# Two transitions with two norms each: fewer weight slabs rounded on the way, the normed rows recorded in two parts, sums over two tiles at a time

## The chip, the cores and the metric

The kernel runs on one core of a Trainium2 chip. The time is that of the device, in microseconds (us), for one execution; lower is better. TensorE (PE in the profile) multiplies, VectorE (DVE) and ScalarE (ACT) do elementwise work, GpSimd (POOL) does elementwise work that touches no PSUM, and SyncE (SP) issues the DMAs. Each engine takes its instructions in the order in which the kernel wrote them, and waits at an instruction until the semaphores that it names have been raised.

## The reference, cut to what matters

One layer of a first network (a mixer with three branches, then a gated feed-forward part), followed by two layers of a second network, on 512 positions of width 1024. Of all this the change touches the places between the parts, where a norm closes one and a norm opens the next:

```python
x = x + rms_norm(merged @ w_o, g_post_mix)      # transition "f": norm 1 (N1) of the product
hf = rms_norm(x, g_pre_ffn)                     #   and norm 2 (N2) of the new x
f_gate, f_up = jnp.split(hf @ w_ffn_in, 2, axis=-1)
f = (jax.nn.silu(f_gate) * f_up) @ w_ffn_out
x = x + rms_norm(f, g_post_ffn)                 # transition "a0": N1 of the product,
h = rmsnorm(x, norm_w) * (1.0 + scale) + shift  #   N2 of the new x, then layer 0 of network 2
proj = h @ w_in
...
x = x + gate * (merged @ w_out)                 # transition "a1": one norm only, to layer 1
```

`rms_norm(x, g)` is `x * rsqrt(mean(x * x) + EPS) * g` over the width.

## The kernel before, in words

Activations are held transposed: a tile is 128 of the 1024 width rows by 512 positions, so a width-1024 array is 8 tiles (k = 0 to 7), and a mean over the width is a sum over partitions and tiles. Each product is computed to near fp32 accuracy from two parts, a rounded one and a rest (`Hhi`, `Hlo` of the activations, `w_hi`, `w_lo` of the weights), in three matmuls per tile (`tile_sums`). The weights arrive as slabs of 8 tiles of 128x128: a DMA brings `w_raw`, ACT rounds it to `w_hi` (`round_weights`), and POOL subtracts to get `w_lo` (`rest_weights`), in pieces of `n` of the slab's 8 tiles. `cut_to(s, n)` records this for all slabs up to s; `self.cut` is the next slab not yet rounded. Slots are few (four in the ring, one called `w_fifth`, and two or three more at a transition, `wf`, `wa`).

A recording layer decides the order: a generator per product yields as it goes, and background tasks (`later`) count these yields down and record a piece of their own work when their count is spent (`tick`). `yield 12` in a task thus means: twelve steps of the product later; in `halves` a step is two tiles.

A transition (`both`) computes the last parts of the old product in two halves of 256 positions, half 0 and half 1 (`halves(first_parts)`), and then the first four parts of the next product, half 0 and half 1 (`halves(next_parts, deep=4)`), where the four parts share each activation tile k. After each half of the old product its task `two_norms` starts:

- `norm_end(N1)`: PE sums the squares over partitions (matmuls with `ones`, `row_sums`), ACT takes the root (`root`, writes `rstds`), DVE inverts it (`inverse`), PE spreads it over the partitions (transposes with `ident`, `row_spread`).
- `onto`: for each tile k, DVE multiplies O by the inverse root (`o_times`) and adds it to `XR` (`x_add`); ACT squares the new x (`square`), and POOL adds the square to N2's accumulator (`add_square`, the second norm has `by="pool"`; tile 7 is not added but summed directly by PE).
- `norm_end(N2)`, the same for the second norm.
- `normed`: for each tile k, DVE scales x (`h_scaled`, tile `hu`), ACT rounds it to `Hhi` (`h_rounded`), and DVE or, for k = 3, 5 and 7, POOL makes `Hlo` (`h_rest`). Three buffers `hu` take turns. In a0 there is a shift too: ACT adds it (`n<-n,mod`) before POOL's rows.

The accumulator of N2 is `nt_178` in the listings of f. In half 1 of the old product every slab that is finished (`over` counts them) lets the next be rounded, from the second one on in `both` (`early=1`). Before the next product's half 0 the task of half 0 is recorded to its end (`self.finish(tasks[0])`).

Of the kernel before, what the change touches and what calls it, by code (L numbers as in the profile page):

```python
# [171 lines left out]
def program(nc, A, out):  # L172
# [202 lines left out]
    class Order:  # L375
# [172 lines left out]
                        done -= 512  # L548
                        yield 1

        def halves(self, parts, before=None, after=None, deep=1, early=2):
            kept, over = {}, 0
            for h, c in enumerate(HALF):
                for n0 in range(0, len(parts), deep):
                    group = range(n0, n0 + deep)
                    if h == 0 and deep > 1:
                        for n in group:
                            for k in parts[n][1]:
                                kept[n, k] = self.tile(calm=True)
                    if before and n0 == 0:  # L560
                        before(h)
                    if h and deep > 1 and n0 == 0:
                        self.cut_to(self.cut + 1)
                    bank = [open_[h] if open_ else self.wide.take() for _, _, _, _, open_ in parts[n0:n0 + deep]]
                    for x, k in enumerate(parts[n0][1]):
                        for n in group:
                            X, ks, key, evac, open_ = parts[n]
                            if h == 0 and deep == 1:
                                kept[n, k] = self.tile()
                            b, tile, ends = bank[n - n0], kept[n, k], k == ks[-1]  # L570
                            names = [(*key, c.start)] * ends + [("slab", tile.s)] * (h and tile.ends)
                            self.tile_sums(banks[b][:, 0:256], tile, X, k, c, k == ks[0] and not open_, ends, self.freed[b], names)
                            if h and tile.ends:
                                self.slab_done(tile.s)
                                self.old = self.sent
                                self.send()
                                over += 1
                                if deep == 1 and over > early:
                                    self.cut_to(self.cut, 4)
                            if (x * deep + n) % 2:  # L580
                                yield 1
                            if ends:
                                X.spent = sums.by(*key, c.start)
                                self.freed[b] = evac(banks[b][:, 0:256], sums.by(*key, c.start), c)
                if after:
                    after(h)
# [44 lines left out]
        def normed(self, c, N, x_ready, hs, scale, shift, H_free, *before, by=None, gap=0, odds=(4, 6)):  # L631

            gone = [None] * len(hs)
            h = c.start // 256

            def rest(k, odd):
                who = (by or "pool") if odd else "dve"
                self.h_rest(N, k, c, hs[k % len(hs)], shift and shift(k), odd, who)
                done = (dve_norm if who == "dve" else pool_norm).by("rest", N.name, k, h)
                gone[k % len(hs)] = done  # L640
                self.H.h[k] = tuple(act_norm.by("h", N.name, k, i) if i <= h else None for i in range(2))
                old = self.H.l[k]
                self.H.l[k] = (done, None) if h == 0 else (old[0], done)

            for k in range(KT):
                if k == 2 and gap:
                    yield gap
                t = hs[k % len(hs)]
                self.h_scaled(N, k, c, t, scale(k), [N.m, x_ready(k, c), gone[k % len(hs)], before])
                if k:  # L650
                    rest(k - 1, k in odds)
                self.h_rounded(N, k, c, t, shift and shift(k), [H_free, before])
            self.norm_read(N, dve_norm.by("scaled", N.name, KT - 1, h))
            rest(KT - 1, True)
# [432 lines left out]

        def onto(self, c, name, dst, o_ready, N1, N2, x_ready, *before):
            h = c.start // 256
            for k in range(KT + 1):  # L1090
                if k < KT:
                    self.o_times(name, dst, k, c, N1, [N1.m, o_ready[k, h]])
                if k:
                    self.x_add(name, dst, k - 1, c, before)
                    x_ready[k - 1, h] = dve_o.by("x", name, k - 1, h)
                    self.norm_add(N2, k - 1, XR[:, k - 1, c], x_ready[k - 1, h], c)
            self.norm_read(N1, dve_o.by("times", name, KT - 1, h))

        def two_norms(self, h, name, dst, o_ready, N1, N2, x_ready, hs, scale, shift, H_free, *before):
            c = HALF[h]  # L1100
            yield 2 if h else 1
            yield from self.norm_end(N1, c, 3 if h else 1)
            self.onto(c, name, dst, o_ready, N1, N2, x_ready, *before)
            yield 9 if h else 12
            yield from self.norm_end(N2, c, 1 if h else 3)
            yield from self.normed(c, N2, lambda k, c: x_ready[k, c.start // 256], hs, scale, shift, H_free, *before, gap=8)

        def both(self, first_parts, next_parts, chain, name, *slots_free):
            self.pump()
            self.ready_sqrt()  # L1110
            self.wide.past(self.main.which)
# [2 lines left out]
            self.send()  # L1114
            self.retire(slots)
            H_free = self.H.spent
            self.run(self.halves(first_parts, after=lambda h: tasks.append(self.later(chain(h, H_free))), early=1))
            self.run(self.halves(next_parts, before=lambda h: self.finish(tasks[h]), deep=4))
            self.main.past([self.wide.which[(self.wide.turn - 1) % 8]])
            return self.gone(slots)  # L1120

# [200 lines left out]
        def walk(self):  # L1322
# [119 lines left out]
            for n in range(3):  # L1442
# [2 lines left out]
                [(MS, range(KT), ("o", n), evac(n), None) for n in range(3, KT)],  # L1445
                [(H, range(KT), ("raw", i, x), (lambda o, done, c, i=i, x=x: self.raw(i, x, o, done, c)), None) for i in range(2) for x in range(2)],
                lambda h, H_free: self.two_norms(h, "O", O, o_ready, n_post, n_pre, x_ready, hu[h], lambda k: P("g_pre_ffn", k), None, H_free, x_again),
                "f", Y.spent)
            norm_done += [H.h[KT - 1][1], H.l[KT - 1][1]]
            F = Split(each(Fhi), each(Flo), FT)  # L1450
            for i in range(2):
# [85 lines left out]
        def layer(self, L, H, x_ready, x_parts, x_chain, x_slots_free, layer_free):  # L1537
# [3 lines left out]
            begun = self.both(x_parts,  # L1541
                              [(H, range(KT), (t, L, 0, g), (self.to_k if t == "bk" else self.to_q)(L, 0, g), None)
                               for t, g in (("bk", 0), ("bk", 1), ("bk", 2), ("bq", 0))],
                              x_chain, f"a{L}", *x_slots_free)
            x_free = dict(x_ready)
            begun += [H.h[KT - 1][1], H.l[KT - 1][1]]
            self.begun = begun
# [704 lines left out]
    class Dve(Order):  # L2252
# [316 lines left out]

        def o_times(self, name, dst, k, c, N1, points):  # L2570
            self.wait_ge(*points)
            self.tt(dst[:, k, c], dst[:, k, c], N1.r, ALU.mult).then_inc(*dve_o("times", name, k, c.start // 256))

        def x_add(self, name, dst, k, c, points):
            h = c.start // 256
            self.wait_ge(dve_o.by("times", name, k, h), *points)
            self.tt(XR[:, k, c], XR[:, k, c], dst[:, k, c], ALU.add).then_inc(*dve_o("x", name, k, h))

        def first_gated(self, i):
            self.wait_ge(act_ffn.by("tanh", i))  # L2580
# [445 lines left out]
```

## Time and profile before

| | |
|---|---|
| median of 3 runs | 2541.43 us (2541.1 to 2542.52) |
| the profiled execution | 2543.01 us, of which its span is 2541.2 us |
| PE busy | 2497.3 us, 98% of the span |
| POOL busy | 1152.4 us, 45% |
| DVE busy, ACT busy | 1167.8 us, 1060.3 us |

Read it as follows: PE is busy nearly throughout, and the other engines less than half of the time, so the kernel's time is PE's work plus what PE waits. The average says nothing of a single transition, in which short dependent steps go round all four engines.

### The profile page before, as it was taken

To read this page: it belongs to the slowest core of one execution; us is meant where nothing else is said; L and a number is where in the kernel's file an instruction comes from. 1 tells how busy PE (TensorE), PEld (TensorE's weight loads), DVE (VectorE), ACT (ScalarE), POOL (GpSimd) and SP (SyncE) were. 2 spreads that over 40 slices of the span, in tenths; PEclk is the share of its full clock that TensorE was granted. 3 is DMA by queue.
4 is the path that set the end of the run, shared out by engine and by line. 5 is a ranking of instruction groups with operands and counts; after the bars stand their busy time and mean duration, and the time that the engine had idled before them with its cause. 6 is when DMAs were issued, how large, how long until landed. Compare 5 with 4: busy or idle time off the path is not lost.

```text
span 2541.2 us, 33038 instructions
## 1 busy us (share of the span) xinstructions
PE 2497.3 (98%) x13246; PEld 2145.8 (84%) x13246; DVE 1167.8 (46%) x2376; ACT 1060.3 (42%) x2026; POOL 1152.4 (45%) x682
## 2 busy tenths in 40 slices
PE   8999999999999999999999999999999999999998
PEld 7788888888888888889888888888898888898887
DVE  7672477755415782104243455522243345544313
ACT  4472498952325332325433333333344333333322
POOL 4354354554446355445444445534444334444442
PEclk9999999999999999999999999999999999999999
DMA  5223211035433453222222222222322222222222
GB/s 201 67 100 109 68 42 34 34 116 199 154 115 113 159 194 124 100 100 75 99 83 83 83 79 87 92 83 99 115 84 84 83 83 75 92 79 88 92 100 75
DMA packets 71769, 250.47 MB, mean 99 GB/s; under 512 B 7872, under 2 KB 12736, under 8 KB 71232
## 3 DMA queue, kind: packets, MB, share of 16 engines
q1 hardware_dynamic: 71616, 248.35, 28.2%
q8 instruction: 105, 1.72, 0.3%
q14 instruction: 48, 0.39, 0.0%
HBM read 246.22 MB, written 2.10 MB: 98 GB/s over the span
## 4 chain that ended last, share of the span: by engine, by line
PE 86%; DVE 6%; ACT 5%; POOL 1%; issue 1%; DMA 0%; SPq 0%; DVEq 0%; ACTq 0%; POOLq 0%
PE bank L1736 84%; PE bank L1746 2%; ACT PP L1954 1%; POOL w_lo L2802 1%; ACT pt_hi L1954 1%; ACT QQ L1954 1%; ACT w_hi L1954 1%; DVE pt_lo L2256 0%; DVE rk_lo L2256 0%; DVE nt L2256 0%; DVE Y L2256 0%; DVE XR L2256 0%; DVE C L2256 0%; DVE PP L2509 0%; DMA XR<-in_x 0%
## 5 line engine op out<-in xcount | busy, mean ns | idle before, releaser
L2802 POOL TENSOR_TENSOR w_lo<-w_raw,w_hi 128x1024 fp32r<-128x1024 f32 (+1 forms) x319 | 761.7, 2392 | 882.3 <-ACT w_hi L1954 882.0
L1736 PE MATMUL bank<-Hhi,w_hi 128*128 128x512 f32 (+1 forms) x1676 | 656.5, 392 | 4.5 <-DVE XC L2264 4.5
L1736 PE MATMUL bank<-Hhi,w_lo 128*128 128x512 f32 (+1 forms) x1676 | 647.6, 386 | 0.0
L1736 PE MATMUL bank<-Hlo,w_hi 128*128 128x512 f32 (+1 forms) x1676 | 647.5, 386 | 0.0
L1954 ACT ACTIVATE w_hi<-w_raw 128x1024 fp32r<-128x1024 f32 (+1 forms) x319 | 326.1, 1027 | 123.1 <-DMA w_raw<-in_wa 81.7
L1736 PEld LDWEIGHTS bank<-Hhi,w_lo 128*128 128x128 f32 x1676 | 315.6, 188 | 65.0
L1736 PEld LDWEIGHTS bank<-Hhi,w_hi 128*128 128x128 f32 x1676 | 316.0, 189 | 61.5 <-DVE XC L2264 4.9
L1736 PEld LDWEIGHTS bank<-Hlo,w_hi 128*128 128x128 f32 x1676 | 316.4, 189 | 56.1
L2802 POOL TENSOR_TENSOR w_fifth_lo<-w_fifth_raw,w_fifth_hi 128x1024 fp32r<-128x1024 f32 (+1 forms) x79 | 190.7, 2415 | 224.8 <-ACT w_fifth_hi L1954 224.8
L1736 PE MATMUL bank<-Hhi,w_fifth_hi 128*128 128x512 f32 x404 | 162.6, 402 | 0.0
L1736 PE MATMUL bank<-Hhi,w_fifth_lo 128*128 128x512 f32 x404 | 157.9, 391 | 0.0
L1736 PE MATMUL bank<-Hlo,w_fifth_hi 128*128 128x512 f32 x404 | 157.7, 390 | 0.0
L2827 POOL TENSOR_SCALAR PP<-PP,small 128x128 f32<-128x128 f32 (+3 forms) x128 | 65.8, 533 | 75.3 <-DVE small L2256 74.9
L1736 PE MATMUL bank<-Y,w_hi 128*128 128x512 f32 x304 | 93.5, 389 | 0.0
L1954 ACT ACTIVATE w_fifth_hi<-w_fifth_raw 128x1024 fp32r<-128x1024 f32 (+1 forms) x79 | 81.6, 1036 | 26.5 <-DMA w_fifth_raw<-in_wa 21.2
L1736 PE MATMUL bank<-w_hi,Hhi 128*128 128x256 f32 (+2 forms) x296 | 89.9, 304 | 0.0
L1736 PEld LDWEIGHTS bank<-Hhi,w_fifth_lo 128*128 128x128 f32 x404 | 75.8, 188 | 16.6
L1736 PE MATMUL bank<-w_hi,Hlo 128*128 128x256 f32 (+2 forms) x296 | 89.6, 303 | 0.0
L1736 PE MATMUL bank<-w_lo,Hhi 128*128 128x256 f32 (+2 forms) x296 | 89.5, 302 | 0.0
L1736 PEld LDWEIGHTS bank<-Hhi,w_fifth_hi 128*128 128x128 f32 x404 | 76.0, 188 | 12.5 <-issue 0.2
L1736 PEld LDWEIGHTS bank<-Hlo,w_fifth_hi 128*128 128x128 f32 x404 | 76.2, 189 | 12.3
L2539 DVE CUSTOM_DVE_ANT_0 wm<-wm,c 128x1024 f32<-128x1024 f32 x48 | 78.8, 1646 | 6.6 <-DMA wm<-in_w_ada 6.4
(413 smaller groups left out, 4913.6 us busy)
## 6 DMA issues: line engine op xcount, KB each, us to landing
w_raw<-in_wb SPq DMA_DIRECT2D x169, 512.0 KB, 3.4
w_raw<-in_wa SPq DMA_DIRECT2D x139, 512.0 KB, 3.3
wm<-in_w_ada SPq DMA_DIRECT2D x48, 512.0 KB, 4.4
w_fifth_raw<-in_wb SPq DMA_DIRECT2D x42, 512.0 KB, 3.4
w_fifth_raw<-in_wa SPq DMA_DIRECT2D x35, 512.0 KB, 3.2
wa_raw<-in_wb SPq DMA_DIRECT2D x5, 512.0 KB, 5.3
XR<-in_x SPq DMA_DIRECT2D x4, 512.0 KB, 8.1
w1k<-in_w1k SPq DMA_DIRECT2D x1, 2048.0 KB, 12.5
```

The lines of the kernel that those rows point to most:

```text
L1736: return self.e.matmul(o, lhs, rhs, start=start, stop=stop)
L1746: return self.e.transpose(o, i, ident[0:n, 0:n])
L1954: return self.e.activation(o, a, func, **kw)
L2539: self.e.tensor_tensor_reduce(x, x, cc[l][:, :], .5, 0., ALU.mult, ALU.add, mod[:, l, n:n + 1]).then_inc(*dve_mod("row", l, n))
L2802: self.e.tensor_tensor(x.lo[:, k:k + n, :], x.raw[:, k:k + n, :], f(x.hi[:, k:k + n, :]), ALU.subtract).then_inc(*w_rest(s, k))
L2827: self.e.tensor_scalar(p, p, r[:, n:n + 1], 1., ALU.mult, ALU.mult).then_inc(*pool_nsa("p", u, n))
```

## The change

In `halves`, slabs are rounded in half 1 of the old product only when `over` is in `cuts`: 2 in f and a1, 2 and 3 in a0. Two slabs more are rounded inside `two_norms` of half 1, between `norm_end(N1)` and `onto`. `normed` gives way for 3 steps before row 4 of half 0; before the next product only rows 0 to 3 need have been recorded. `o_times` and `x_add` work on two tiles at once. The sums of half 0's second norm are recorded two steps earlier, and its spread one step earlier still.

```diff
-        def halves(self, parts, before=None, after=None, deep=1, early=2):
+        def halves(self, parts, before=None, after=None, deep=1, cuts=()):
...
-                                if deep == 1 and over > early:
+                                if over in cuts:
                                     self.cut_to(self.cut, 4)
...
             for k in range(KT):
                 if k == 2 and gap:
                     yield gap
+                if k == 4 and h == 0:
+                    yield 3
+                self.emitted = k + 1
...
         def onto(self, c, name, dst, o_ready, N1, N2, x_ready, *before):
             h = c.start // 256
-            for k in range(KT + 1):
-                if k < KT:
-                    self.o_times(name, dst, k, c, N1, [N1.m, o_ready[k, h]])
-                if k:
-                    self.x_add(name, dst, k - 1, c, before)
-                    x_ready[k - 1, h] = dve_o.by("x", name, k - 1, h)
-                    self.norm_add(N2, k - 1, XR[:, k - 1, c], x_ready[k - 1, h], c)
-            self.norm_read(N1, dve_o.by("times", name, KT - 1, h))
+            for k in range(0, KT, 2):
+                self.o_times(name, dst, k, c, N1, [N1.m, o_ready[k, h], o_ready[k + 1, h]])
+                self.x_add(name, dst, k, c, before)
+                for j in (k, k + 1):
+                    x_ready[j, h] = dve_o.by("x", name, k, h)
+                    self.norm_add(N2, j, XR[:, j, c], x_ready[j, h], c)
+            self.norm_read(N1, dve_o.by("times", name, KT - 2, h))
...
             yield from self.norm_end(N1, c, 3 if h else 1)
+            if h:
+                self.cut_to(self.cut + 1)
             self.onto(c, name, dst, o_ready, N1, N2, x_ready, *before)
-            yield 9 if h else 12
-            yield from self.norm_end(N2, c, 1 if h else 3)
+            yield 9 if h else 10
+            yield from self.norm_end(N2, c, 1 if h else 2)
...
-            self.run(self.halves(first_parts, after=lambda h: tasks.append(self.later(chain(h, H_free))), early=1))
-            self.run(self.halves(next_parts, before=lambda h: self.finish(tasks[h]), deep=4))
+
+            def before(h):
+                if h:
+                    self.finish(tasks[1])
+                    return
+                while self.emitted < 4:
+                    tasks[0][1] = next(tasks[0][0])
+
+            self.emitted = 0
+            self.run(self.halves(first_parts, after=lambda h: tasks.append(self.later(chain(h, H_free))), cuts=cuts))
+            self.run(self.halves(next_parts, before=before, deep=4))
```

How this moves instructions is shown at three places, all in transition f; a0 has the same pattern. First POOL's order, from the last two additions of half 0's second norm (`nt_178`) to the first two of half 1's. Before:

```order
L2807 TENSOR_TENSOR nt_178<-nt_178,nt_176 128x256
L2802 TENSOR_TENSOR w_lo<-w_raw,w_hi 128x512 x4
L2802 TENSOR_TENSOR w_fifth_lo<-w_fifth_raw,w_fifth_hi 128x512 x2
L2802 TENSOR_TENSOR w_lo<-w_raw,w_hi 128x512 x2
L2813 TENSOR_TENSOR Hlo<-hu_179,Hhi 128x256
L2813 TENSOR_TENSOR Hlo<-hu_181,Hhi 128x256
L2813 TENSOR_TENSOR Hlo<-hu_180,Hhi 128x256
L2807 TENSOR_TENSOR nt_178<-nt_178,nt_175 128x256
```

The same place on POOL after the change:

```order
L2823 TENSOR_TENSOR nt_178<-nt_178,nt_176 128x256
L2818 TENSOR_TENSOR w_lo<-w_raw,w_hi 128x512 x2
L2829 TENSOR_TENSOR Hlo<-hu_179,Hhi 128x256
L2829 TENSOR_TENSOR Hlo<-hu_181,Hhi 128x256
L2829 TENSOR_TENSOR Hlo<-hu_180,Hhi 128x256
L2818 TENSOR_TENSOR w_lo<-w_raw,w_hi 128x1024
L2818 TENSOR_TENSOR w_fifth_lo<-w_fifth_raw,w_fifth_hi 128x1024
L2823 TENSOR_TENSOR nt_178<-nt_178,nt_175 128x256
```

Three slabs' worth of rests have left the place ahead of half 0's `Hlo` rows 3, 5 and 7, and two whole slabs stand now between row 7 and half 1's additions.

Second ACT's order, from the last rounded rows of half 0 to the first square of half 1's second norm (`nt_178<-XR`); `rstds<-bank` is the root of half 1's first norm. Before:

```order
L1954 ACTIVATE Hhi<-hu_181 128x256
L1954 ACTIVATE Hhi<-hu_179 128x256
L1954 ACTIVATE Hhi<-hu_180 128x256
L1954 ACTIVATE Hhi<-hu_181 128x256
L1954 ACTIVATE Hhi<-hu_179 128x256
L1954 ACTIVATE Hhi<-hu_180 128x256
L1954 ACTIVATE rstds<-bank,eps 128x2
L1954 ACTIVATE nt_178<-XR 128x256
```

The same place on ACT after the change:

```order
L1968 ACTIVATE Hhi<-hu_181 128x256
L1968 ACTIVATE Hhi<-hu_179 128x256
L1968 ACTIVATE rstds<-bank,eps 128x2
L1968 ACTIVATE Hhi<-hu_180 128x256
L1968 ACTIVATE Hhi<-hu_181 128x256
L1968 ACTIVATE Hhi<-hu_179 128x256
L1968 ACTIVATE Hhi<-hu_180 128x256
L1968 ACTIVATE w_hi<-w_raw 128x1024
L1968 ACTIVATE w_fifth_hi<-w_fifth_raw 128x1024
L1968 ACTIVATE nt_178<-XR 128x256
```

The root has moved ahead of rows 4 to 7, and two roundings stand ahead of the squares.

Third PE's order in half 1 of the old product of f, at the sums (`ones`) of half 0's second norm; `w_fifth` and `w` are two slabs, one behind the other. Before:

```order
L1736 MATMUL bank<-MShi,w_lo 128x256
L1736 MATMUL bank<-ones,nt_178 128x1 x2
L1736 MATMUL bank<-ones,nt_177 128x1 x2
L1736 MATMUL bank<-MShi,w_hi 128x256
L1736 MATMUL bank<-MSlo,w_hi 128x256
```

After the change:

```order
L1750 MATMUL bank<-MShi,w_fifth_lo 128x256
L1750 MATMUL bank<-ones,nt_178 128x1 x2
L1750 MATMUL bank<-ones,nt_177 128x1 x2
L1750 MATMUL bank<-MShi,w_hi 128x256
L1750 MATMUL bank<-MSlo,w_hi 128x256
```

The sums stood behind the third tile of slab `w` and stand now ahead of its first: three tiles (nine matmuls) earlier, and four tiles in a0. The spread that belongs to them has moved along; nothing else has moved on PE in any transition. On DVE the 16 products and 16 sums over 256 positions in each of f and a0 have become half as many over 2x256; on SP nothing has moved.

## Rows read from the trace of the kernel before

**Rows 1.** The page: span, and busy time by engine.
```profile
span 2541.2 us, 33038 instructions
...
PE 2497.3 (98%) x13246; PEld 2145.8 (84%) x13246; DVE 1167.8 (46%) x2376; ACT 1060.3 (42%) x2026; POOL 1152.4 (45%) x682
```

**Rows 2.** Timeline of PE in f: start, busy, instruction, idle before it and its releaser.
```profile
804.02 0.95 PE L1736 MATMUL bank<-ones,nt 128*128 128x1 f32 x8
...
809.93 0.28 PE L1736 MATMUL bank<-MShi,w_lo 128*128 128x256 f32 x1
811.15 0.35 PE L1736 MATMUL bank<-Hhi,wf_hi 128*128 128x256 f32 x1 [0.94 <-ACT Hhi L1954]
...
813.03 0.95 PE L1736 MATMUL bank<-ones,nt 128*128 128x1 f32 x8
...
818.28 0.43 PE L1746 MATMUL bank<-ident,rstds 128*128 128x128 f32 x2 [2.05 <-DVE rstds L2290]
...
826.23 1.05 PE L1736 MATMUL bank<-ones,nt 128*128 128x1 f32 x8 [1.05 <-POOL nt L2807]
```

**Rows 3.** Timeline of PE in a0.
```profile
1176.77 0.95 PE L1736 MATMUL bank<-ones,n 128*128 128x1 f32 x8
...
1182.54 0.28 PE L1736 MATMUL bank<-Hhi,wa_hi 128*128 128x256 f32 x1
...
1190.71 0.43 PE L1746 MATMUL bank<-ident,rstds 128*128 128x128 f32 x2 [3.42 <-DVE rstds L2290]
...
1198.94 0.95 PE L1736 MATMUL bank<-ones,n 128*128 128x1 f32 x8
```

**Rows 4.** Windows: stretch, its us, PE, PEld, DVE, ACT, POOL, granted clock, DMA.
```profile
1190.00:1200.00 10.00, 9.29 (x66) 9.29 (x67) 6.99 (x17) 3.87 (x11) 5.15 (x7) 0.83 0.00 1
...
1860.00:1870.00 10.00, 10.00 (x86) 10.00 (x85) 4.95 (x12) 4.60 (x10) 6.79 (x6) 1.00 0.31 107
```

**Rows 5.** Timeline of ACT in f, and one row of a0.
```profile
786.43 1.06 ACT L1954 ACTIVATE wf_hi<-wf_raw 128x1024 fp32r<-128x1024 f32 x1
...
817.07 0.81 ACT L1954 ACTIVATE Hhi<-hu 128x256 fp32r<-128x256 f32 x2 [1.41 <-DVE hu L2264]
817.79 0.24 ACT L1954 ACTIVATE rstds<-bank,eps 128x2 f32<-128x2 f32 x1
...
1189.80 0.51 ACT L1954 ACTIVATE n<-n,mod 128x256 f32<-128x256 f32 x1
```

**Rows 6.** Timeline of POOL in f.
```profile
785.81 7.68 POOL L2802 TENSOR_TENSOR wf_lo<-wf_raw,wf_hi 128x1024 fp32r<-128x1024 f32 x3
798.24 5.14 POOL L2807 TENSOR_TENSOR nt<-nt,nt 128x256 f32<-128x256 f32 x6 [4.74 <-ACT nt L1954]
804.47 5.42 POOL L2802 TENSOR_TENSOR w_lo<-w_raw,w_hi 128x512 fp32r<-128x512 f32 x4 [1.09 <-ACT w_hi L1954]
...
815.54 1.59 POOL L2813 TENSOR_TENSOR Hlo<-hu,Hhi 128x256 fp32r<-128x256 f32 x2
...
821.04 5.14 POOL L2807 TENSOR_TENSOR nt<-nt,nt 128x256 f32<-128x256 f32 x6 [2.36 <-ACT nt L1954]
```

**Rows 7.** Timeline of DVE in f.
```profile
779.12 0.69 DVE L2256 TENSOR_TENSOR nt<-nt,nt 128x512 f32<-128x512 f32 x1 [4.75 <-ACT nt L1954]
783.67 10.11 DVE L2256 TENSOR_TENSOR nt<-nt,nt 128x256 f32<-128x256 f32 x4 [3.86 <-ACT nt L1954]
...
797.29 0.42 DVE L2256 TENSOR_TENSOR XR<-XR,O 128x256 f32<-128x256 f32 x1
...
799.51 0.63 DVE L2256 TENSOR_TENSOR XR<-XR,O 128x256 f32<-128x256 f32 x1
...
831.18 0.87 DVE L2264 SCALAR_TENSOR_TENSOR hu<-XR,par,bank 128x256 f32<-128x256 f32 x2
```

**Rows 8.** Timeline of POOL in a0.
```profile
1170.99 5.16 POOL L2807 TENSOR_TENSOR n<-n,n 128x256 f32<-128x256 f32 x6 [7.15 <-ACT n L1954]
...
1193.46 5.14 POOL L2807 TENSOR_TENSOR n<-n,n 128x256 f32<-128x256 f32 x6 [2.35 <-ACT n L1954]
```

More of the change, by code:

```diff
@@ L1102, in two_norms, with both @@
             yield from self.norm_end(N1, c, 3 if h else 1)
+            if h:
+                self.cut_to(self.cut + 1)
             self.onto(c, name, dst, o_ready, N1, N2, x_ready, *before)
-            yield 9 if h else 12
-            yield from self.norm_end(N2, c, 1 if h else 3)
+            yield 9 if h else 10
+            yield from self.norm_end(N2, c, 1 if h else 2)
             yield from self.normed(c, N2, lambda k, c: x_ready[k, c.start // 256], hs, scale, shift, H_free, *before, gap=8)
-        def both(self, first_parts, next_parts, chain, name, *slots_free):
+        def both(self, first_parts, next_parts, chain, name, cuts, *slots_free):
             self.pump()
@@ L1447, in walk @@
                 lambda h, H_free: self.two_norms(h, "O", O, o_ready, n_post, n_pre, x_ready, hu[h], lambda k: P("g_pre_ffn", k), None, H_free, x_again),
-                "f", Y.spent)
+                "f", (2,), Y.spent)
             norm_done += [H.h[KT - 1][1], H.l[KT - 1][1]]
@@ L1543, in layer @@
                                for t, g in (("bk", 0), ("bk", 1), ("bk", 2), ("bq", 0))],
-                              x_chain, f"a{L}", *x_slots_free)
+                              x_chain, f"a{L}", (2,) if L else (2, 3), *x_slots_free)
             x_free = dict(x_ready)
@@ L2571, in o_times @@
             self.wait_ge(*points)
-            self.tt(dst[:, k, c], dst[:, k, c], N1.r, ALU.mult).then_inc(*dve_o("times", name, k, c.start // 256))
+            x = dst[:, k:k + 2, c]
+            self.tt(x, x, N1.r.unsqueeze(1).broadcast_to([128, 2, 256]), ALU.mult).then_inc(*dve_o("times", name, k, c.start // 256))
         def x_add(self, name, dst, k, c, points):
@@ L2576, in x_add @@
             self.wait_ge(dve_o.by("times", name, k, h), *points)
-            self.tt(XR[:, k, c], XR[:, k, c], dst[:, k, c], ALU.add).then_inc(*dve_o("x", name, k, h))
+            x = XR[:, k:k + 2, c]
+            self.tt(x, x, dst[:, k:k + 2, c], ALU.add).then_inc(*dve_o("x", name, k, h))
         def first_gated(self, i):
```

## The prediction

> **What bounds the kernel now.** I read the page first: PE is busy 2497.3 of 2541.2 us [rows 1], so what counts is where PE waits, and in a transition who releases it. The timelines of PE show this. In f it idles 0.94 us for the first `Hhi`, 2.05 us for the spread of half 1's first norm and 1.05 us for half 1's second sums [rows 2]; in a0 it idles 3.42 us for the same spread, and none at the second sums [rows 3]. The other timelines say who is late. Half 1's root stands on ACT behind all eight `Hhi` rows of half 0: the root starts at 817.79, right behind the pair of 817.07, though PE's sums for it stood at 813.03 [rows 2, 5]. The rows themselves wait for POOL, whose `Hlo` rows start only at 815.54, behind the roundings that began at 804.47 [rows 6]. And PE's wait at 826.23 ends with POOL's six additions, 821.04 plus 5.14 us [rows 2, 6]. In a1 PE is busy without a gap in half 1 (10.00 of 10.00 us) [rows 4].
>
> After a transition PE has no slack to recover what it lost, so the shift at half 1's second sums, 826.23 in f and 1198.94 in a0, is what reaches the end. I price both.
>
> **Unit costs.** 86 matmuls fit into 10.00 us [rows 4], 0.12 us each: a tile is 0.36 us, the four tiles of one k 1.44. The block of eight `ones` matmuls: 0.95 busy, 0.9 from start to start [rows 2]. Root, inverse, spread: from 817.79 to 818.28 [rows 2, 5], 0.5. DVE scales a row in 0.39 (two in 0.87 busy, which overlap) [rows 7]. ACT rounds a row in 0.41 [rows 5]. A sum over 256 positions shows 0.42 busy, 0.34 apart; one over 512 shows 0.69 [rows 7], so I take 0.6 for a pair. POOL: 2.4 to 2.56 for a whole slab (7.68 for three) [rows 6], I take 2.4; an addition 0.885 apart (5.14 for six, the last 0.74) [rows 6].
>
> **Half 0's sums earlier.** PE reaches them in f at 804.02 less 9 x 0.12, 802.94 [rows 2]. POOL's additions ended at 803.38 [rows 6]. With pairs the third square comes a little later than it did, since x arrives in twos (two more 0.3 us steps, partly hidden behind POOL): I take 0.4 late, 803.8. PE waits 0.85 there. In a0: 1176.77 less 1.44 is 1175.33, and POOL is ready at 1170.99 + 5.16 + 0.4 = 1176.55: 1.2 [rows 3, 8]. The old product of f then ends 0.85 later, at 810.05 + 0.85 = 810.9 instead of 810.05 (last matmul 809.93) [rows 2]. As the rows are ready by then, the 0.94 us wait disappears: H begins at 810.9 instead of 811.15. In a0, where nothing was idle, it begins at 1182.54 + 1.2 = 1183.75 [rows 3].
>
> **The root out of the queue.** After one k (1.44) and the sums (0.9) ACT can take the root: 813.25 in f, 1186.1 in a0; only rows 0 to 3 stand ahead of it, and those are done. The inverse is there at 813.75 and 1186.6, and PE asks for the spread six tiles after the sums, 2.16 us: 815.4 and 1188.25. The waits of 2.05 and 3.42 are gone. PE is 2.9 us ahead of before in f and 2.5 in a0 at this point. The 18 tiles that follow (6.5 us) bring it to half 1's second sums at 822.2 and 1195.0.
>
> **The roundings in front of half 1's additions.** Now the other side. Rows 4 to 7 of half 0 follow the inverse. In f they take four scalings and two rests on DVE, 2.65 us with one wait for ACT: 816.4. In a0 ACT is the longer one, four rows at 0.41 and three shifts at 0.51 [rows 5] less overlap, 3.1 us: 1189.7. Only then do ACT and POOL come to the two whole slabs. This work stood elsewhere before and cost nothing there but the waits above; POOL is now idle between 807 and 812 us and busy afterwards.
>
> How long it takes depends on how DVE and POOL get on when both read two tensors of SBUF. In the trace four such DVE sums over 256 positions, next to whole-slab rests on POOL, took 10.11 us, 2.5 each, against 0.42 alone [rows 7]: each waited out one POOL instruction. Next to POOL's short additions it was 0.63 [rows 7]. That speaks for taking turns, one whole instruction each. The Trainium skill (SBUF — State Buffer, the part on the shared port pair) says the same as a rule: it is an exclusive lock held for the whole instruction, and the later one fully blocks. By that rule the taking of turns below would hold for the pairs, which nothing in the trace of before shows, and the sum is the first one; if the engines merely slowed each other, it is the second.
>
> - Taking turns, f: POOL's row 7 ends at 817.15, the first `x_add` pair 0.6 later, 817.75; then slab 2.4, pair 0.6, slab 2.4, pair 0.6: 823.75; one addition 0.74, the last pair 0.6, five additions at 0.885: 829.5. Against 826.19 that is **+3.3**.
> - Taking turns, a0: row 7 ends at 1190.5, first pair 1191.1, slab-pair-slab-pair 1197.1, addition and pair 1198.45, five additions 1202.85. PE's sums stood at 1198.94 [rows 3]: **+3.9**.
> - Without turns, f: ACT's rounding (1.06 busy, 0.96 apart [rows 5]) lets POOL start at 817.4, two slabs 822.2, six additions 827.5: +1.3. In a0: 1190.7, 1195.5, 1200.8: +1.9.
>
> I take the first, since its 2.5 us rows are of the same two kinds of instruction. PE would idle about 7.3 us in f and 7.9 in a0.
>
> **The clock.** After 3.42 us of idleness in a0 the granted clock is 0.83 over the next 10 us [rows 3, 4]: a third of that stretch at the lower of its two levels (1.2 instead of 2.4 GHz), 1.7 us lost. After 2.05 us in f nothing of the kind came; the stretch shows its matmuls at the usual spacing [rows 2]. With 7 us of idleness I expect the loss in f too, **+1.7**, and in a0 the same again in place of the old one, 0. Bounds: no new loss, or twice as much in each.
>
> **What costs nothing.** The 16 instructions fewer on DVE in each of f and a0 save perhaps 0.06 each, on an engine that waits for POOL here anyway. One slab fewer is rounded ahead at the end of f and a0, and two in a1; PE needs 24 matmuls over 512 positions per slab after the transition, at twice 0.12 some 5.5 us, and POOL 2.4, so the cover is four rounded slabs; gone, it would cost 2.4. In a1 a sum of half 1 now stands ahead of rows 4 to 7 and delays them by about 1.2 us; they are not needed until the old product is finished, some 4 us later, and PE shows no gap [rows 4].
>
> **Sum.** 3.3 + 3.9 + 1.7 = 8.9 us. The profiled execution took 2543.01 us with a span of 2541.2 and would become 2551.9; against the median of the runs, 2541.43, it gives **2550.3 us**.
>
> **Rivals.**
> - *The engines only slow each other* (second sum, 1.3 + 1.9 = 3.2, or 4.9 with the clock in f): 2544.6 to 2546.3, not to be told from no change, which is 0.2% or 5.1 us here. For it: `x_add` at 0.63 next to short additions reads as sharing too. Against it: the 10.11 us row.
> - *The roundings slip in before half 1's additions matter*, and the change is faster. It decides at the start of the additions: earlier than 821.04 in f and 1193.46 in a0 [rows 6, 8]. Working back 4.8 for POOL and about 1.0 for ACT, half 0's row 7 would have to be rounded by 815.2 and 1187.6; I have 816.4 and 1189.7. If the two slabs cost nothing at all, the additions would end near 824.0 and 1196.7, 2.2 less each, and a0's 1.7 of lower clock might go: 6.1 us, 2535.3 us. For it: the root's waits really vanish. Against it: the order on POOL, which is strict.
> - *Slabs run short after the transition*: one or two waits of 2.4 us on top of the sum, 2552.7 to 2555. Little speaks for it, as POOL needs less than half of PE's time per slab.
>
> **How the numbers follow.** Taking turns 0.55, slowing each other 0.25, faster 0.12, short slabs 0.08. Low end: the second sum, without the delay at half 0's sums (0.85 and 1.2), is about 1.2 us, 2542.6; I go down to 2542. High end: 8.9 with twice the clock loss in each transition, 3.4 more: 2553.7; I take 2554. Slower by over 0.2% needs more than 5.1 us: taking turns nearly always, short slabs, and a small part of the sharing case: 0.64. Within 0.2%: 0.25. Faster: 0.11.
>
> **What would show it.** In the profile after: no wait of PE for `rstds` of half 1's first norm (right: the root left the queue). A wait of 0.5 to 1.3 us at half 0's second sums. The largest wait of each transition at half 1's second sums, released by POOL's `nt` or `n`, 5 us and more. Whole-slab `w_lo` on POOL from about 817.5 and 1191, with `x_add` rows of 2 us and more beside it: turns; of 1 us: sharing. A stretch of lower clock behind both. Wrong would be: the second sums of half 1 earlier than 826.23 and 1198.94.

## The result, and the profile after

| | median us | lowest to highest | ratio to the kernel before, 95% interval |
|---|---|---|---|
| kernel before, beside it | 2541.10 | 2540.14 to 2542.52 | |
| changed kernel | 2557.15 | 2555.14 to 2557.32 | 1.0057 [1.0047, 1.0068] |

The change makes the kernel slower: by 0.57% or 14.5 us as the ratio has it, by 16 us as the two medians have it. The page's lines that answer to [rows 1]:

```profile
span 2555.5 us, 32988 instructions
...
PE 2503.3 (98%) x13246; PEld 2152.7 (84%) x13246; DVE 1163.3 (46%) x2344; ACT 1058.9 (41%) x2019; POOL 1155.3 (45%) x675
```

The span grew by 14.3 us and PE's busy time by 6.0 with the same 13246 instructions. So some 8 us are waits of PE, and the 6 us in which the same instructions were busy longer I put down to a slower clock, which the windows below show. To find the places I measure from spread to spread: the pair of `ident` matmuls of half 0's first norm stands in each transition at the same place of PE's order.

| us | start to f | f to a0 | a0 to a1 | a1 to end |
|---|---|---|---|---|
| before | 795.54 | 372.75 | 682.36 | 690.55 |
| after | 796.32 | 379.55 | 690.36 | 689.27 |
| difference | +0.78 | **+6.80** | **+8.00** | -1.28 |

I leave the outer columns out. The first grew by a longer time at the lower clock before 100 us, far ahead of any changed instruction. The last lost such a stretch: in a1 the granted clock was 0.72 from 1850 to 1856 us before, behind a wait of 0.79 us, and 1.00 from 1866 to 1872 us after, behind a wait of 0.80 us. The rest is in f and a0. PE's rows in both, after (timeline, to be read against [rows 2, 3]; `nt` is f, `n` is a0):

```profile
805.41 1.05 PE L1750 MATMUL bank<-ones,nt 128*128 128x1 f32 x8 [1.53 <-POOL nt L2823]
807.72 0.63 PE L1760 MATMUL bank<-ident,rstds 128*128 128x128 f32 x2
...
818.38 0.38 PE L1760 MATMUL bank<-ident,rstds 128*128 128x128 f32 x2
831.74 1.87 PE L1750 MATMUL bank<-ones,nt 128*128 128x1 f32 x8 [6.52 <-POOL nt L2823]
...
1185.12 1.05 PE L1750 MATMUL bank<-ones,n 128*128 128x1 f32 x8 [2.05 <-POOL n L2823]
...
1195.41 0.95 PE L1750 MATMUL bank<-ones,n 128*128 128x1 f32 x8
...
1212.56 1.87 PE L1750 MATMUL bank<-ones,n 128*128 128x1 f32 x8 [7.26 <-POOL n L2823]
```

The waits of 2.05 and 3.42 us for `rstds` are gone: the root left the queue. In their place stand 1.53 and 2.05 us at half 0's second sums and 6.52 and 7.26 us at half 1's, all released by POOL. The 1.87 us of the eight `ones` matmuls, 0.95 at full clock, shows what follows such a wait. In windows (stretch, its us, PE, PEld, DVE, ACT, POOL, granted clock, DMA):

```profile
800.00:815.00 15.00, 13.47 (x101) 13.27 (x100) 7.18 (x15) 7.48 (x21) 7.29 (x8) 0.89 0.38 130
...
830.00:845.00 15.00, 13.26 (x86) 13.05 (x87) 5.40 (x14) 6.51 (x15) 6.63 (x7) 0.74 0.01 2
```

The same windows before:

```profile
800.00:815.00 15.00, 13.90 (x114) 13.32 (x114) 10.90 (x20) 10.84 (x28) 13.48 (x12) 1.00 0.44 145
830.00:845.00 15.00, 15.00 (x112) 14.35 (x112) 4.79 (x12) 7.16 (x15) 4.63 (x4) 1.00 0.17 54
```

A clock of 0.89 over 15 us is a fifth to a quarter of it at the lower level. The chain that makes PE wait, on POOL and then on DVE (timelines of f, after):

```profile
798.99 6.37 POOL L2823 TENSOR_TENSOR nt<-nt,nt 128x256 f32<-128x256 f32 x6 [4.71 <-ACT nt L1968]
...
820.33 2.64 POOL L2818 TENSOR_TENSOR w_lo<-w_raw,w_hi 128x1024 fp32r<-128x1024 f32 x1 [0.21 <-ACT w_hi L1968]
822.92 2.86 POOL L2818 TENSOR_TENSOR w_fifth_lo<-w_fifth_raw,w_fifth_hi 128x1024 fp32r<-128x1024 f32 x1
825.73 5.95 POOL L2823 TENSOR_TENSOR nt<-nt,nt 128x256 f32<-128x256 f32 x6
```

```profile
820.00 0.69 DVE L2270 TENSOR_TENSOR XR<-XR,O 128x512 f32<-128x512 f32 x1
820.61 0.68 DVE L2270 TENSOR_TENSOR O<-O,bank 128x512 f32<-128x512 f32 x1
821.32 2.20 DVE L2270 TENSOR_TENSOR XR<-XR,O 128x512 f32<-128x512 f32 x1
823.44 0.68 DVE L2270 TENSOR_TENSOR O<-O,bank 128x512 f32<-128x512 f32 x1
824.15 2.17 DVE L2270 TENSOR_TENSOR XR<-XR,O 128x512 f32<-128x512 f32 x1
```

Two `x_add` pairs (`XR<-XR,O`) begin while POOL is in a whole slab and last until it is through it, 2.2 us against 0.69: the two take turns. And POOL's six additions take 6.37 and 5.95 us, where [rows 6] shows 5.14 twice. In a0 half 0's six take longer too, where [rows 8] shows 5.16:

```profile
1178.54 6.53 POOL L2823 TENSOR_TENSOR n<-n,n 128x256 f32<-128x256 f32 x6 [7.29 <-ACT n L1968]
```

### The profile page after: what moved, and what is told of

It reads as the page before. It is cut to its first block, busy times and chain, and to the rows that moved or that the text cites. A ratio compares the mean times of both kernels' runs of the same rounds, so it can differ in the third digit from the quotient of the medians.

```text
span 2555.5 us, 32988 instructions
## 1 busy us (share of the span) xinstructions
PE 2503.3 (98%) x13246; PEld 2152.7 (84%) x13246; DVE 1163.3 (46%) x2344; ACT 1058.9 (41%) x2019; POOL 1155.3 (45%) x675
## 4 chain that ended last, share of the span: by engine, by line
PE 87%; DVE 6%; ACT 5%; POOL 1%; issue 1%; DMA 0%; SPq 0%; DVEq 0%; POOLq 0%; ACTq 0%
PE bank L1750 85%; PE bank L1760 2%; ACT PP L1968 1%; ACT pt_hi L1968 1%; ACT QQ L1968 1%; ACT w_hi L1968 1%; DVE pt_lo L2270 0%; DVE rk_lo L2270 0%; POOL n L2823 0%; POOL nt L2823 0%; DVE nt L2270 0%; DVE Y L2270 0%; DVE C L2270 0%; DVE PP L2523 0%; POOL w_lo L2818 0%
## 5 line engine op out<-in xcount | busy, mean ns | idle before, releaser
L2818 POOL TENSOR_TENSOR w_fifth_lo<-w_fifth_raw,w_fifth_hi 128x1024 fp32r<-128x1024 f32 x77 | 190.6, 2475 | 224.6 <-ACT w_fifth_hi L1968 224.6
L1968 ACT ACTIVATE w_fifth_hi<-w_fifth_raw 128x1024 fp32r<-128x1024 f32 x77 | 81.4, 1057 | 25.0 <-DMA w_fifth_raw<-in_wa 20.9
```

Source lines behind the costliest of these rows:

```text
L1968: return self.e.activation(o, a, func, **kw)
L2818: self.e.tensor_tensor(x.lo[:, k:k + n, :], x.raw[:, k:k + n, :], f(x.hi[:, k:k + n, :]), ALU.subtract).then_inc(*w_rest(s, k))
```

## Experiments

The change has five edits: fewer cuts; half 0's rows in two parts; half 0's second sums sooner; pairs; two slabs ahead of half 1's additions. E1 to E3 take one off the changed kernel, E4 leaves only the first two, E5 and E6 make one of these two alone in the kernel before, E7 to E9 add one of the other three to E4. E10 to E12 try to go on from E6. Each median is over 9 or 10 executions; the kernel before stood at 2542.1 to 2542.5 beside them. The changed kernel was not run beside them: where they are set against it, its 2557.15 is that of the result, beside which the kernel before stood at 2541.10. Each ratio carries about 0.1% (2.5 us) either way, so a difference of 2 or 3 us between two kernels of this table is not clear of noise.

| | kernel | median us | ratio to before, 95% interval |
|---|---|---|---|
| E1 | changed, no slabs ahead | 2546.88 | 1.0015 [1.0006, 1.0024] |
| E2 | changed, no pairs | 2549.25 | 1.0024 [1.0015, 1.0034] |
| E3 | changed, sums late | 2549.42 | 1.0027 [1.0017, 1.0037] |
| E4 | fewer cuts, two parts | 2537.08 | 0.9977 [0.9967, 0.9988] |
| E5 | before, two parts | 2540.93 | 1.0001 [0.9991, 1.0010] |
| E6 | before, fewer cuts | 2536.89 | 0.9982 [0.9973, 0.9992] |
| E7 | E4, sums early | 2539.64 | 0.9990 [0.9981, 1.0000] |
| E8 | E4, pairs | 2541.65 | 0.9997 [0.9987, 1.0006] |
| E9 | E4, slabs ahead | 2546.43 | 1.0016 [1.0007, 1.0026] |
| E10 | E6, no cuts | 2549.79 | 1.0030 [1.0021, 1.0040] |
| E11 | E6, half 1's sums later | 2537.42 | 0.9978 [0.9969, 0.9988] |
| E12 | E6, products in pairs | 2537.93 | 0.9986 [0.9977, 0.9996] |

**E1, the slabs.**

```diff
-            if h:
-                self.cut_to(self.cut + 1)
             self.onto(c, name, dst, o_ready, N1, N2, x_ready, *before)
```

> The changed kernel without the two slabs that are rounded ahead of half 1's additions; nothing is left out of the computation, the slabs are rounded at their old places behind. Theory A (the slabs stand in front of the additions and take turns with DVE, and this is the main part of the loss): in f and in a0 the sums over half 1's additions are ready some 4 us earlier, the waits of 6.5 and 7.3 us of PE there go to 2 to 3, and the lower clock behind them goes in part; time about 2546 us (8 to 13 less than the changed kernel's 2557.15). Theory B (the pairs and the early sums of half 0 are the main part): less than 4 us less, 2553 or more. Theory C (the slabs are needed by the product that follows, and are short when rounded later): a new wait on w_hi or w_lo in the next product, and a time above 2557.

2546.88 us, 10.3 less: theory A. PE's rows at the second sums (timeline; the last is that of a0):

```profile
804.99 1.05 PE L1748 MATMUL bank<-ones,nt 128*128 128x1 f32 x8 [1.52 <-POOL nt L2821]
...
827.48 1.87 PE L1748 MATMUL bank<-ones,nt 128*128 128x1 f32 x8 [2.69 <-POOL nt L2821]
...
1204.48 1.05 PE L1748 MATMUL bank<-ones,n 128*128 128x1 f32 x8 [3.45 <-POOL n L2821]
```

The waits at half 1's fell by 3.8 us in each, and those at half 0's stayed. PE waits for weights twice in the whole run, 3.0 and 1.1 us, both at the start of the kernel (9.1 and 10.6 us), where the kernel before waits too; in the transitions there is no such wait, so theory C falls as well. But 4.4 us over the kernel before are left, which no slab explains.

**E2, the pairs.** `onto`, `o_times` and `x_add` as before the change:

```diff
-            for k in range(0, KT, 2):
-                self.o_times(name, dst, k, c, N1, [N1.m, o_ready[k, h], o_ready[k + 1, h]])
-                self.x_add(name, dst, k, c, before)
...
+            for k in range(KT + 1):
+                if k < KT:
+                    self.o_times(name, dst, k, c, N1, [N1.m, o_ready[k, h]])
+                if k:
+                    self.x_add(name, dst, k - 1, c, before)
...
```

> The changed kernel with the additions and the products with N1's row one tile at a time, as before; nothing is left out of the computation. Theory A (pairs let POOL's additions of squares begin later and run longer, since squares come in bursts of two and DVE's pair writes hold POOL up): half 0's six additions fall from 6.4 to 6.5 us back to 5.1 to 5.3, PE's waits of 1.53 us in f and 2.05 us in a0 at half 0's second sums fall to 0.3 to 0.9, and the time is about 2553 us (3 to 6 less than the changed kernel's 2557.15). Theory B (pairs cost nothing, the burst is hidden): 2556 to 2558. Theory C (pairs save): above 2558.

2549.25 us, 7.9 less: theory A in kind, and above its 3 to 6. POOL's six additions are back at 5.15 us (798.05) and PE waits 0.34 us at half 0's second sums:

```profile
803.25 1.05 PE L1751 MATMUL bank<-ones,nt 128*128 128x1 f32 x8 [0.34 <-POOL nt L2822]
...
827.59 1.87 PE L1751 MATMUL bank<-ones,nt 128*128 128x1 f32 x8 [5.32 <-POOL nt L2822]
```

The clock between 800 and 815 us is 1.00 again, and I take that for what my 3 to 6 had too little of. It is not certain to come with these waits: E7 has them too (0.33 us, and 0.51 for the spread behind) and its clock there is 0.89.

**E3, the early sums.**

```diff
-            yield 9 if h else 10
-            yield from self.norm_end(N2, c, 1 if h else 2)
+            yield 9 if h else 12
+            yield from self.norm_end(N2, c, 1 if h else 3)
```

> The changed kernel with half 0's second sums at their old place, two steps of products later, and the spread three steps behind them; nothing is left out of the computation. Theory A (the sums are asked for before POOL has them, at a clock price too): PE's waits of 1.53 us in f and 2.05 us in a0 before half 0's second sums fall to 0.5 or less, and the two-part rows still keep the root out of PE's queue: time about 2553.5 us (3 to 4 less than the changed kernel's 2557.15). Theory B (the waits at half 0's sums are made up for by the wait at half 1's, which POOL ends at a time that PE does not set): 2556.5 to 2557.5, with the wait at half 1's sums longer by what is saved. Theory C (the early sums bring the root earlier): above 2558.

2549.42 us, 7.7 less, twice what theory A gave. PE waits 0.46 at half 0's second sums and the clock is 1.00 from 800 to 815 us. The wait at half 1's stayed at 6.52 us in f, so theory B falls: what PE loses at half 0's sums puts half 1's first norm off by as much, and with it the chain that ends in half 1's second sums. Counted from f's first spread, half 1's first sums stand at 16.41 us against 19.01 in the changed kernel, and its second sums at 32.82 against 35.42: 2.6 us sooner both.

**E4, what is left.** E1, E2 and E3 in one.

> The changed kernel without the slabs ahead of half 1's additions, without the pairs and without the early sums: what is left of the change is the fewer cuts and the normed rows in two parts; nothing is left out of the computation. Theory A (the rows in two parts take away the waits of 2.05 and 3.42 us on the root, and the rest of the change is what costs): 2536 to 2539 us, 2 to 5 below the kernel before. Theory B (half 1's additions are next to be late, so the time saved at the root is given back there): 2540 to 2543, no difference to the kernel before. Theory C (fewer cuts leave slabs short in the next product): 2543 or more, with waits on w_hi or w_lo.

2537.08 us: theory A by the time, 5.4 below the kernel before. That the two parts are the reason is what E5 and E6 test.

**E5, the rows in two parts alone.**

```diff
                 if k == 2 and gap:
                     yield gap
+                if k == 4 and h == 0:
+                    yield 3
+                self.emitted = k + 1
```

and `both` with its `before` of the change.

> The kernel before with one part of the change alone: half 0's normed rows issued in two parts around half 1's root; cuts as before; nothing is left out of the computation. Theory A (the rows in two parts carry the whole gain of the run that has only them and the fewer cuts, because they take PE's waits of 2.05 and 3.42 us on the root away): PE's waits on rstds fall as in that run, 2536 to 2539 us, some 5 below the kernel before. Theory B (the fewer cuts carry the gain, by leaving DVE and POOL free of slabs near the additions): 2541 to 2543, no difference to the kernel before. Theory C (without the fewer cuts a slab comes to lie in front of the root): the wait on rstds stays, and the time is within 1 us of the kernel before.

2540.93 us, ratio 1.0001: theory B. The wait of half 1's spread on `rstds` is gone, as theory A wanted it, and yet the time stays. From f to a0 it is 372.76 us against 372.75. Where the wait went (timeline of PE, f and a0):

```profile
824.25 1.07 PE L1748 MATMUL bank<-ones,nt 128*128 128x1 f32 x8 [2.43 <-POOL nt L2819]
...
1196.74 1.47 PE L1748 MATMUL bank<-ones,n 128*128 128x1 f32 x8 [3.57 <-POOL n L2819]
```

Half 1's root runs sooner, but its additions stand on DVE behind half 0's rows 4 to 7 as before; POOL begins them at 819.08, which is 0.9 us sooner when the 1.1 us by which this run's f came sooner are taken off. So one wait of 2.43 us at the sums stands for the old ones of 2.05 and 1.05. From f to a0 PE idles 1.06 us less than before and is busy 1.07 us longer: its clock was 0.89 from 815 to 830 us, and 1.00 before.

```profile
815.00:830.00 15.00, 12.57 (x91) 12.16 (x90) 10.85 (x27) 6.92 (x19) 6.19 (x9) 0.89 0.00 1
```

**E6, the fewer cuts alone.**

```diff
-                                if deep == 1 and over > early:
+                                if over in cuts:
                                     self.cut_to(self.cut, 4)
```

with the `cuts` of the change handed to it.

> The kernel before with one part of the change alone: cuts only at the second (and, in a0, third) slab that the old product gives back; nothing is left out of the computation. Theory A (fewer roundings alone move no wait of PE, the root is late by its place in the queues): PE's waits of 2.05 and 3.42 us on rstds stay, 2541 to 2544 us. Theory B (the roundings that lay ahead of the root made it late): these waits fall by over 1 us each and the time to 2539 or less.

2536.89 us: theory B. f to a0 is 369.15 us, 3.6 less than before. The waits on `rstds` fell from 2.05 to nothing and from 3.42 to 1.02 us, with the root still behind all eight rows of half 0 on ACT (it starts at 814.05, against 817.79 before). POOL and PE in f:

```profile
804.34 2.73 POOL L2802 TENSOR_TENSOR w_lo<-w_raw,w_hi 128x512 fp32r<-128x512 f32 x2 [1.09 <-ACT w_hi L1954]
811.54 0.72 POOL L2813 TENSOR_TENSOR Hlo<-hu,Hhi 128x256 fp32r<-128x256 f32 x1 [4.47 <-ACT Hhi L1954]
```

```profile
811.34 0.95 PE L1736 MATMUL bank<-ones,nt 128*128 128x1 f32 x8
814.55 0.43 PE L1746 MATMUL bank<-ident,rstds 128*128 128x128 f32 x2
...
822.50 1.05 PE L1736 MATMUL bank<-ones,nt 128*128 128x1 f32 x8 [1.05 <-POOL nt L2807]
```

In [rows 6] POOL was in weights without a gap until 815.54, and the rows of half 0, ahead of the root on ACT, had to wait for it. Now it does one slab, and takes the first of its `Hlo` rows at 811.54, 4 us sooner.

**E7, E8, E9: the other three, one at a time on E4.**

> The kernel with the fewer cuts and the rows in two parts, and in addition half 0's second sums asked for two steps sooner, with single additions and no slab ahead of half 1's; nothing is left out of the computation. Theory A (the early sums cost only what PE waits for POOL, 0.3 and 0.7 us by the run with single additions, and a little at half 1 behind): 2538 to 2540 us, 1 to 3 more than the 2537.1 of the kernel without them. Theory B (the early sums cost by themselves what they did in company, 7.7 us): 2544 to 2545. Theory C (sooner sums bring the root sooner, a gain): 2536 or less.

2539.64 us, +2.6: theory A by the time. The waits at half 0's second sums are the 0.33 and 0.70 us that it named, but behind them the clock fell in f, which no theory had:

```profile
800.00:815.00 15.00, 14.16 (x106) 13.94 (x106) 8.39 (x20) 8.06 (x23) 4.46 (x5) 0.89 0.34 111
```

> The kernel with the fewer cuts and the rows in two parts, and in addition the sums of two tiles at a time, with half 0's second sums at their old place and no slab ahead of half 1's; nothing is left out of the computation. Theory A (pairs make POOL's six additions 6.4 us instead of 5.1 in both halves, of which half 0's late sums hide nearly all and half 1's none): PE's waits at half 1's second sums grow from 1.6 and 2.3 us to 2.7 and 3.5, and the time is 2539 to 2542 us, 2 to 5 more than 2537.1. Theory B (pairs cost the 7.9 us that they cost in company): 2544 to 2546. Theory C (pairs cost nothing by themselves): 2536 to 2538.

2541.65 us, +4.6: theory A. What pairs do is seen in two grouped rows, POOL's additions and DVE's `x_add` in f (name, count, shortest/median/longest ns, first and last start). The kernel before:

```profile
L2807 POOL TENSOR_TENSOR nt<-nt,nt x12: 723/738/747, 798.2 to 825.5; 128x256 f32<-128x256 f32 x12
```

```profile
L2256 DVE TENSOR_TENSOR XR<-XR,O x16: 418/628/955, 796.6 to 824.6; 128x256 f32<-128x256 f32 x16
```

E8:

```profile
L2821 POOL TENSOR_TENSOR nt<-nt,nt x12: 721/920/1182, 798.4 to 823.9; 128x256 f32<-128x256 f32 x12
```

```profile
L2268 DVE TENSOR_TENSOR XR<-XR,O x8: 691/692/694, 796.8 to 820.7; 128x512 f32<-128x512 f32 x8
```

Singly it is DVE that is held up (0.42 becomes 0.63 and more) and POOL never; in pairs it is POOL (0.74 becomes up to 1.18) and DVE never. DVE is through half 0's additions 1.3 us sooner (801.50 against 802.79), but the sums wait for POOL, which is through 1.4 us later (804.74 against 803.38).

> The kernel with the fewer cuts and the rows in two parts, and in addition the slabs that are rounded ahead of half 1's additions; single additions, half 0's second sums at their old place; nothing is left out of the computation. Theory A (turns: each whole slab's rest on POOL holds one or two of DVE's additions up until it is done, whatever the size of the addition): XR's additions beside it last over 2 us, half 1's second sums come 3 to 4 us later in f and in a0 with the lower clock behind them, 2543 to 2548 us, 6 to 11 more than 2537.1. Theory B (shared: DVE and POOL slow each other, and the turns of 2.2 us are of the pairs): 1.3 to 1.9 us later each, 2539 to 2542. Theory C (the slabs are worth nothing or a gain when additions are single): 2538 or less.

2546.43 us, +9.4: theory A. DVE beside POOL, f:

```profile
817.10 2.36 DVE L2271 TENSOR_TENSOR XR<-XR,O 128x256 f32<-128x256 f32 x1
819.38 0.41 DVE L2271 TENSOR_TENSOR O<-O,bank 128x256 f32<-128x256 f32 x1
819.71 2.29 DVE L2271 TENSOR_TENSOR XR<-XR,O 128x256 f32<-128x256 f32 x1
```

```profile
816.77 2.41 POOL L2817 TENSOR_TENSOR w_lo<-w_raw,w_hi 128x1024 fp32r<-128x1024 f32 x1 [0.20 <-ACT w_hi L1969]
819.13 2.60 POOL L2817 TENSOR_TENSOR w_fifth_lo<-w_fifth_raw,w_fifth_hi 128x1024 fp32r<-128x1024 f32 x1
```

A single addition is held as long as a pair was. The product into `O`, one input of which is in a bank, took 0.41 in the middle of POOL's slab (819.38).

**E10, no cuts at all.** E6 with both lists of cuts empty.

> The kernel before with no cuts at all during half 1 of the old product (the changed kernel keeps one in f and a1 and two in a0); the rest as before; nothing is left out of the computation. Theory A (each slab rounded there delays half 1's chain, so fewer still is better): the rest of the wait on the root in a0 (1.02 us) goes, 2532 to 2536 us. Theory B (what is not rounded there is missing in the next product, which asks for it at once): waits on w_hi, w_lo or their parts at the start of the next product of over 2 us each, 2540 or more. Theory C (nothing left to win): within 1 us of 2536.9.

2549.79 us, 12.9 over E6: theory B. PE waits for weights where the next product begins, in f:

```profile
811.23 0.38 PE L1736 MATMUL bank<-Hhi,w_hi 128*128 128x256 f32 x1 [0.71 <-ACT w_hi L1954]
813.66 0.39 PE L1736 MATMUL bank<-Hlo,w_hi 128*128 128x256 f32 x1 [2.04 <-POOL w_lo L2802]
```

In a0 there are three, 1.07, 2.05 and 1.49 us. So one cut (two in a0) is better than none and better than the kernel before's number; other numbers were not tried.

**E11, half 1's second sums two steps later.**

```diff
-            yield 9 if h else 12
+            yield 11 if h else 12
```

> The kernel before with the fewer cuts, and in addition half 1's second sums two steps of products later; nothing is left out of the computation. Theory A (the wait of 1.05 us at these sums is filled with products, but the chain that ends in half 1's first H starts at the same instant, as POOL sets it, so the wait appears at the first Hhi): within 1.5 us of 2536.9. Theory B (PE's wait is what counts, so filling it gains it and the lower clock of 0.5 to 0.77 behind it in a0): 2533 to 2535. Theory C (sums later mean root and rows later by two steps, 1.4 us at each place): 2538 to 2541.

2537.42 us: theory A. PE no longer waits at the sums, but 0.55 us at the spread and 1.02 us in f and 1.28 in a0 at the first `Hhi` of half 1, where E6 waits 0.32 and 0.28. POOL sets the time of these sums, and where PE waits for what hangs on them is all one.

**E12, products in pairs, additions singly.**

```diff
+            for k in range(0, KT, 2):
+                self.o_times(name, dst, k, c, N1, [N1.m, o_ready[k, h], o_ready[k + 1, h]])
+                for j in (k, k + 1):
+                    self.x_add(name, dst, j, c, before)
...
```

> The kernel before with the fewer cuts (2536.9 us), and in addition the products with N1's row two tiles at a time while the additions onto XR stay one tile at a time; nothing is left out of the computation. Theory A (what holds POOL's additions up is the long addition onto XR, whose two inputs are both in SBUF, not the product, one of whose inputs is in a bank): POOL's additions stay at 0.74 us each and 5.1 to 5.4 for six, no new wait at the sums, 2535 to 2538 us. Theory B (squares that come in bursts of two are what stretches POOL's six additions): 6.0 us or more for six, 2539 to 2543.

2537.93 us: theory A by the time, though its "no new wait" did not quite hold: the waits at half 1's second sums are 1.59 and 1.60 us, in E6 1.05 and 1.04. POOL's additions in f take 0.738 us at the median and 0.917 at most (0.920 and 1.182 in E8), so it is mainly the long addition with both inputs in SBUF that slows POOL. From first to last the six take 6.0 us all the same, as theory B said, because the second waits 0.81 for its square; busy they are 5.2. Nothing is gained over E6.

## Why the prediction was wrong

The direction was right and the size too small: 2550.3 us, with an upper end of 2554, against 2557.15. Step by step, with times of after moved back by what had piled up ahead (0.78 us in f, 7.58 in a0):

| step | predicted f / a0 | found f / a0 |
|---|---|---|
| wait at half 0's second sums | 0.85 / 1.2 | 1.53 / 2.05 |
| waits on the root | gone | gone |
| half 1's first spread | 815.4 / 1188.25 | 817.60 / 1190.88 |
| `x_add` beside a slab | 2 us and more | 2.20 / 2.19 |
| half 1's second sums | 829.5 / 1202.85 | 830.96 / 1204.98 |
| shift there | +3.3 / +3.9 | +4.7 / +6.0 |
| clock on top | +1.7 / 0 | +2.1 / +2.0 |

By this table the shifts and the clock come to 14.8 us, where the prediction had 8.9. Two steps failed.

**The first is "Half 0's sums earlier".** Its "0.4 late" took POOL's additions as 5.14 us, begun a little later. With pairs they are 6.4 and 6.5 us, since POOL waits for DVE's pairs; they end 1.2 us late in f and 1.3 in a0, and PE's waits are 0.7 and 0.85 us longer than predicted. I had the rule of turns in hand and applied it in one direction only, to DVE. The larger part is that no lower clock was set down behind these waits. It came, 0.89 from 800 to 815 us and 0.91 from 1170 to 1190 us, with 1.00 in both before. Half 1's first spread stood 2.2 and 2.6 us later than predicted: what the longer waits leave of this, 1.5 and 1.8 us, is the clock. E2 and E3 each take most of the wait away (0.34 and 0.46 us are left in f, 0.70 and 0.61 in a0), their clock there is 1.00, and each gives back 7.7 to 7.9 us of the 16. The same error of turns lies in the five additions at 0.885 behind the slabs, but it is small: 5.95 us for the six, where the sum has 5.8 with a pair between them.

**The second is the clock behind half 1's sums in a0**, "the same again in place of the old one, 0". Found: 2.0 us. Before's stretch of lower clock lay ahead of 1198.94 ([rows 4], 1190 to 1200 us) and was already in that time, so that a new one behind the sums is all loss.

**The main mechanism was right.** "Taking turns" against "the engines only slow each other" is settled by 2.20 us here and 2.36 in E9, and the Trainium skill's rule (SBUF — State Buffer, the shared port pair) agrees with both. The term was too large: 829.5 less 824.0 and 1202.85 less 1196.7 put half 1's second sums off by 11.6 us for the slabs. Counted from the first spread of each transition, they were put off by 3.8 us in f and in a0, 7.6 together, both from E1 to the changed kernel and from E4 to E9; with the clock behind it that cost 10.3 and 9.4 us. Here luck helped the number: what was too much for the slabs hid part of what was missing ahead of them. The kernel without their cost was to have these sums at 824.0 and 1196.7 and to take 2535.3 us. E1, which is that kernel, has them at 827.1 and 1201.2, on the same count, and takes 2546.9.

**"What costs nothing" held one gain.** Fewer roundings were priced as a debt only. E6 shows them worth 5.2 us; I had seen that POOL's `Hlo` rows waited "behind the roundings that began at 804.47" [rows 6], and still put the gain down to the rows in two parts, which alone give nothing (E5). The size was about right (2.9 in f and 2.5 in a0 against 5.4 for E4), so this did not move the number, but it named the wrong edit; that the size came out was luck. A slip in the same step entered no term: 24 matmuls at twice 0.12 us are 5.8 us, not 5.5.

**The account.** E4 to the changed kernel is 20.1 us. One at a time on E4: slabs 9.4, pairs 4.6, early sums 2.6, together 16.6. The 3.5 us that remain are not clear of noise, with 2.5 us either way on each ratio. In kind there is something between pairs and early sums: pairs make POOL later, early sums make PE sooner, and only with both are the waits at half 0's second sums 1.53 and 2.05 us (0.33 and 0.70 in E7, 0.47 and 0.61 in E8). That this is worth 3.5 us is not shown; a lower clock came behind the short waits of E7 too. Less the 5.4 us of E4, the 20.1 are 14.7 over the kernel before. The result has 16 by its medians, because the kernel before stood at 2541.10 beside it and at 2542.51 beside E1 to E4.

The rival of short slabs is out for this change: PE's only waits for weights in the changed kernel, 2.0 and 1.1 us, stand at its start (8.6 and 10.0 us), and none in a transition. E10 shows what such waits look like once too few slabs are rounded.

The best kernels here are E4, E6 and E11, 0.2% below the kernel before and not to be told from one another, with E12 about a microsecond behind; E6 is the simplest of them.

## What to carry to other kernels

When two engines take turns on two-input sums, work out who waits for whom in both directions: a longer instruction on one is a longer wait on the other, and it is the one at the end of the chain that counts. A wait that is moved out of one queue is only won if the next link of the same chain was not late as well; look for what stands ahead of the link itself, here weights on POOL, before changing PE's order. A wait can cost more than its length when the clock falls behind it. And such a stretch of lower clock is to be placed before or behind the instant at which one compares, or it is counted twice or not at all.

## What the runs showed of the hardware

- The turns of DVE and POOL depend on where the inputs are. `XR<-XR,O`, both in SBUF, lasts 2.2 to 2.4 us beside a whole slab on POOL, over 256 or 512 positions alike; `O<-O,bank` keeps its 0.41 us there.
- POOL can be the one that waits: an addition of 0.74 us lasted up to 1.18 beside additions of 0.69 on DVE.
- The lower clock does not follow the length of a wait alone. After 1.53 us in the changed kernel's f it came (0.89 from 800 to 815 us), after 2.05 us in f before it didn't ([rows 2]; 1.00), after 1.55 us in E4's f it didn't (1.00), and after 2.33 us in its a0 it did (0.89). The same two waits, 0.33 or 0.34 us and 0.51 us, had it behind them in E7 (0.89 from 800 to 815 us) and not in E2 (1.00). These are single profiled executions. Such a loss is to be given a chance, not a yes or no.
